# Centring two layer-norm tiles on VectorE and six on GpSimd, and one ScalarE table set for logarithm and exponential

## The chip, the cores and the metric

The kernel runs on one core of a Trainium2 chip. The metric is the device time of one execution in microseconds; the time of a kernel is the median of its runs.

The core has five engines that take their instructions in order and wait for each other by semaphores: TensorE (PE in the profile; PEld is its weight load), VectorE (DVE), ScalarE (ACT), GpSimd (POOL) and SyncE (SP, which only issues transfers).

## The reference

Two blocks are computed on one sequence of 512 tokens with 1024 features, in fp32. The first block has two layers of: RMS norm with modulation, an input projection, three mixers side by side (sliding-window attention, retention, gated linear attention), an output projection, an RMS norm and the residual. The second block has two layers, a mixer and a convolutional feed-forward each, and behind each of these four a layer norm:

```python
for l in range(DEPTH):
    y = even_mixer(x, ...) if l % 2 == 0 else odd_mixer(x, ...)
    x = layer_norm(alpha * x + y, ln_g[l, 0], ln_b[l, 0])
    y = conv_ffn(x, ffn_w_up[l], ffn_conv_w[l], ffn_conv_b[l], ffn_w_down[l])
    x = layer_norm(alpha * x + y, ln_g[l, 1], ln_b[l, 1])
return x
```

A layer norm subtracts the mean over the 1024 features from each token, divides by the root of the variance plus 1e-5, and applies a gain and a bias. An inverse root is computed as exp(-0.5 * ln(variance + eps)), so each norm takes one logarithm and one exponential.

## The kernel before

Activations lie transposed: `X` is 8 tiles (k = 0 to 7) of 128 features by 512 tokens. Every matrix product is made of three TensorE passes per weight tile (lines 902 to 904): an operand is split into a high part (`HI`, `WHI`, written by ScalarE) and the rest (`LO`, `WLO`, written by VectorE as a difference of two SBUF tiles). So each product needs ScalarE, then VectorE, then TensorE.

The program is a list of stages, and each engine runs through it with its own instruction stream. The stages that matter here are the four "tails" `even_out`, `down` (layer 0), `odd_out` and `down` (layer 1), each followed by the "head" of the next stage: `up` (0), `odd_in`, `up` (1) and `store`.

At the end of a tail TensorE sums mean and mean of squares over the features (lines 932 to 941). VectorE forms the variance (`RS`, line 2582), copies the mean from PSUM to SBUF (`MEAN`, line 2583), and subtracts it from tiles 0 to 3 (`centred`, line 2045, `N_CENTRED` = 4). Meanwhile ScalarE takes the logarithm (line 1470) and the exponential (line 1472). Then VectorE waits for that result (`rstd_known`).

At the head of the next stage, `normalised` on VectorE goes through the tiles: for k of 4 and more first the centring of tile k (line 2045), then gain times inverse root (`scalar_tensor_tensor`, line 2062), then the low part of tile k-1 (line 2053). Between the last two ScalarE adds the bias and writes the high part (line 1478). In the first three heads TensorE works three output tiles at once, staggered by one input tile (`first_jobs_of`): input step 0 has 3 passes, step 1 has 6, steps 2 to 7 have 9 each. In `store` there are no low parts: the tiles are shifted by ScalarE, transposed by TensorE (line 1429), copied (line 1940) and sent out.

TensorE issues `IDLE` matmuls that nobody reads (line 1443, two passes each) between a tail and the next head, so that it isn't idle there.

The other norms: the stage `out` ends in an RMS norm, `prenorm` (between the two layers of the first block) in another, both by `rstd` (lines 1470, 1472). The stage `mix` (twice) interleaves attention (exponentials, line 1704) with gated linear attention (line 1740 exponential, line 1742 logarithm) and two head norms (lines 1811, 1816 and 1861, 1863). `even_mix` has a head norm too (lines 1666, 1668). A function of ScalarE needs a table set; the build puts an `ACT_TABLE_LOAD` ahead of any function that the loaded set lacks, and `preload_act_table` puts one at a chosen place.

GpSimd issues 22 small loads in the first stages and has nothing after them.

Of the kernel before, what the change touches and what calls it, by code (L numbers as in the profile page):

```python
# [21 lines left out]
ACT = mybir.ActivationFunctionType  # L22
ALU = mybir.AluOpType
# [7 lines left out]
KD = D // P  # L31
# [12 lines left out]
WIDEST = 1280  # L44

NTILES = 34


def t5_bucket(dist):
# [91 lines left out]
def build(nc, io, cst, out, stop=None):  # L141

    ctx = ExitStack()
    with ctx:
# [11 lines left out]
        X = sb("X", [KD, T])  # L156
# [91 lines left out]
        MEAN = STAT[:, 3, :]  # L248
        SQM2 = STAT[:, 2:5:2, :]
        MEAN_PS, MSQ_PS = PS[:, 4, :], PS[:, 5, :]  # L250
# [45 lines left out]
        def sem(name):  # L296
            return ctx.enter_context(nc.semaphore(name))
# [23 lines left out]
            sem(f"at_{n}") for n in ("scores", "scaled", "exp", "probs", "turned", "turn_free", "values", "mixed"))  # L321

        sq_ready, sq_used, rstd_ready, normed = sem("sq_ready"), sem("sq_used"), sem("rstd_ready"), sem("normed")

        sub_sums, sub_rstd, sub_spread = sem("sub_sums"), sem("sub_rstd"), sem("sub_spread")

# [395 lines left out]

        BANKS = {"mod": len(VECTORS) + KD + len(HOT_CUTS), "mix": 4}

        IDLE = {"mod": 5, "prenorm": 6, "out": 7, "even_out": 7, "down": 7, "odd_out": 7, "odd_in": 3}

        HEADS_OF = {("up", 0): 0, ("odd_in", 0): 1, ("up", 1): 2, ("store", 0): 3}
        TAILS = ("out", "even_out", "down", "odd_out")
        HOLDS = ("proj", "even_in", "odd_up")
        N_CENTRED, LAG = 4, 3  # L730
        THREE = [("even_in", 0), ("up", 0), ("odd_in", 0), ("up", 1)]
        BEFORE_THREE = [stages[n - 1] for n in range(1, len(stages)) if stages[n] in THREE]

# [59 lines left out]
        @block.gpsimd  # L793
        def _(pool):
            n_const = [0]

            def load(dst, src):
                n_const[0] += 1
                pool.dma_start(dst, src).then_inc(const_in, 16)

            pool.dma_start(HOT, cst["onehot"]).then_inc(hot_in, 16)
            pool.dma_start(TABLE[0:32, :], io["rel_bias_2"]).then_inc(hot_in, 16)
            pool.wait_ge(pe_met, 1)
            pool.wait_ge(dve_met, 1)
            with nc.allow_non_contiguous_dma(reason="small operands, a feature to a partition"):
                for l in range(LAYERS):
                    load(SINKS[:, 8 * l:8 * l + 8], io["attn_sinks"][l].partition_broadcast(P))
                    for a in range(4):
                        load(GWB[l][32 * a:32 * a + 16, :], io["gla_gate_w"][l])
                    load(GWB[l][16:17, :], io["gla_gate_b"][l:l + 1])  # L810
                    for a in range(2):
                        load(GLAG[64 * a:64 * a + 64, l:l + 1], io["gla_norm_gain"][l].rearrange("(p o) -> p o", o=1))
                load(DECAY, cst["decay"])
                load(UPPER, cst["upper"])
                load(WINDOW, cst["window"])
                load(SUBM, cst["sub"])
                load(HEADS_32, cst["heads"])
                load(LAMP, io["ev_lambda_2"][0].rearrange("a b -> (a b)").partition_broadcast(P))
                N_CONST[0] = 16 * n_const[0]


        @block.sync
# [627 lines left out]
        def _(act):  # L1450
# [73 lines left out]
            def linear(jobs, l, tail=None, late=None, hold=False, early=False, three=False, to_three=False, loads=None):  # L1524
                n, upto = 0, at_split[0] + sum(len(j["chunks"]) for j in jobs if j["kind"] == "F") if hold else len(chunks)
                weights(at_split[0] + 1)
                for i, j in enumerate(jobs):
# [14 lines left out]
                    if j["by"] != "act":  # L1542
                        if j["how"] == "gate" if j["kind"] == "F" else False:
                            gelu(n - 1)
                        me.emptied_by(j["by"])
                        if tail is not None and j["kind"] == "F":
                            if j["n"] == KD - 1:
                                act.preload_act_table(ACT.Ln)
                                weights(at_split[0] + (3 if to_three else 2))
                            act.wait_ge(acc_free_dve, me.emptied["dve"])  # L1550
                            square(SQS[:, j["n"] % 2, :], j["dst"], j["n"], (sq_used, reused(tail, j["n"])))
                        continue
                    if tail is not None and j["n"] == KD - 1:
                        act.preload_act_table(ACT.Ln)
                    bank = take()
                    c = at_split[0]
                    if early and j["kind"] == "F" and c + 1 < len(chunks) and chunks[c + 1][2] - chunks[c - 1][2] <= SLOTS:
# [177 lines left out]
            def state_lane(l):  # L1735
# [89 lines left out]
                inputs(inputs_of("out")[0:3], True)  # L1825
                act.wait_ge(gla_near, NB * (l + 1))
                weights(at_split[0] + 2)
                act.preload_act_table(ACT.Ln)
                gla_mix(NB - 1)
                gla_squares(l)  # L1830
                inputs(inputs_of("out")[3:6], True, 3)
# [34 lines left out]
            for n_met, (s, l) in enumerate(stages, 1):  # L1866
# [6 lines left out]
                if s == "mod":  # L1873
                    for c0, n, src in VECTORS[0]:
                        act.dma_start(VROWS[c0:c0 + n, 0:P], src).then_inc(first_in, 16)
                    act.dma_start(IDN, cst["mats"][:, 0, :]).then_inc(first_in, 16)
                    act.dma_start(z(22).bitcast(I32), io["positions"][0].partition_broadcast(P)).then_inc(pos_in, 16)
                    act.dma_start(TINY[:, 4:7], cst["freq"]).then_inc(pos_in, 16)
                    w_mod = io["w_mod"][0]
                    act.dma_start(MATS[:, 1:8, :], cst["mats"][:, 1:8, :]).then_inc(mats_in, 16)  # L1880
                    for k in (1, 3, 5, 7):
                        act.dma_start(MOD_W[k], w_mod[k * P:k * P + P, 0:2048]).then_inc(mod_loaded[k], 16)
                    act.preload_act_table(ACT.Silu)
                    bank = take()
                    fn(VEC[:, 0:56], bank[:, 0:56], ACT.Copy).then_inc(me.signals(acc_free_act), 1)
                    act.wait_ge(*me.last)
                    fn(CACT, CT, ACT.Silu).then_inc(c_ready, 1)

                    def hot(k):
                        c, w = HOT_CUTS[k]  # L1890
                        bank = take()
                        fn(VECS_SB[:, c:c + w], bank[0:16, 0:w], ACT.Copy, scale=8.0).then_inc(me.signals(acc_free_act), 1)
                    for k in range(HOT_FIRST):
                        hot(k)
                    for k in range(KD):
                        me.emptied_by("dve")
                        act.wait_ge(acc_free_dve, me.emptied["dve"])
                        square(SQM2[:, k % 2, :], X[:, k, :], k, (sq_used, reused(0, k)))
                        if HOT_FIRST + k < len(HOT_CUTS):
                            hot(HOT_FIRST + k)  # L1900
                        if k == 3:
                            act.wait_ge(side_dve, me.after(side_dve, 2))
                        if k in (3, 4):
                            fn(ROPE[:, k - 3, :], z(27 - k), ACT.Sin).then_inc(me.signals(act_step), 1)
                    for group in VECTORS[1:]:
                        c0, n = group[0][0], sum(n for _, n, _ in group)
                        bank = take()
                        fn(VEC[:, c0:c0 + n], bank[:, 0:n], ACT.Copy).then_inc(me.signals(acc_free_act), 1)
                    act.wait_ge(*me.last)
                    act.dma_start(SCR, VECS_SB).then_inc(table_out, 16)  # L1910
                    act.wait_ge(msq_ready, me.after(msq_ready))
                    rstd(RS, MSQ_PS, EPS6)
                    act.wait_ge(mod_used, KD + 3)
                    for j in range(2):
                        r = slice(32 * j, 32 * j + 1)
                        fn(MOD_ROWS[r, :], PS[r, 4, :], ACT.Copy).then_inc(me.signals(mod_rows), 1)
                    weights(2)
# [6 lines left out]
                    act.wait_ge(msq_ready, me.after(msq_ready))  # L1924
                    rstd(RS, MSQ_PS, EPS6)
                elif s == "mix":
                    act.preload_act_table(ACT.Exp)
                    mixers(l)
                elif s in ("even_mix", "odd_mix"):
                    if s == "odd_mix":  # L1930
                        act.preload_act_table(ACT.Exp)
                    attention(UNITS[s])
                elif s == "even_sub":
                    head_squares([H[:, t, :] for t in range(4)], EPS5)
# [36 lines left out]
        def _(dve):  # L1971
# [70 lines left out]
            def centred(k):  # L2042

                dve.wait_ge(*me.last)
                tt(X[:, k, :], X[:, k, :], MEAN, ALU.subtract).then_inc(me.signals(dve_step), 1)  # L2045
# [9 lines left out]
            def normalised(n):  # L2055

                for k in range(KD + 1):
                    if k < KD:
                        if k >= N_CENTRED:
                            centred(k)  # L2060
                        dve.wait_ge(*me.last)
                        stt(X[:, k, :], X[:, k, :], LNG[:, n, k:k + 1], RS, ALU.mult, ALU.mult) \
                            .then_inc(me.signals(normed), 1)
                    if k == 2 and n < 3:
                        weights(at_split[0] + 3)
                    if k and n < 3:
                        low(k - 1, X[:, k - 1, :], LNB[:, n, k - 1:k])
# [389 lines left out]
            for n_met, (s, l) in enumerate(stages, 1):  # L2457
# [71 lines left out]
                else:  # L2529
# [46 lines left out]
                    elif s in TAILS:  # L2576
# [3 lines left out]
                        dve.wait_ge(mean_sq, me.after(mean_sq))  # L2580
                        dve.wait_ge(*me.last)
                        tt(RS, MSQ_PS, MEAN2, ALU.subtract).then_inc(me.signals(var_ready), 1)
                        nc.vector.tensor_copy(MEAN, MEAN_PS).then_inc(me.signals(dve_step), 1)
                        if (s, l) not in BEFORE_THREE:
                            weights(at_split[0] + 2)
                        for k in range(N_CENTRED):
# [48 lines left out]
```

## Time and profile before

| | |
|---|---|
| median of 3 runs | 2103.79 us (2102.29 to 2104.71) |
| the profiled execution | 2098.76 us, its span 2096.8 us |
| TensorE busy | 1991.4 us, 95% of the span |
| VectorE busy | 1089.2 us, 52% |
| ScalarE busy | 959.2 us, 46% |
| GpSimd busy | 12.7 us, 1% |
| granted TensorE clock, mean | 0.981 |

The span is the time between the first and the last instruction of the profiled execution; 2.0 us of its time lie outside. It is 5.0 us shorter than the median of the timed runs.

### The profile page before, as it was taken

The page shows a single profiled execution, that of the slowest core. Times are in us where ns is not written, and L with a number is a line of the kernel's source. Part 1 is how long each engine was busy: PE and PEld are TensorE (multiplying, and loading weights), DVE is VectorE, ACT ScalarE, POOL GpSimd, SP SyncE. Part 2 cuts the span into 40 slices and gives each one's busy share as a digit, 9 for nine tenths or more (in the row PEclk, how much of TensorE's full clock was granted, in tenths as well). Part 3 has the DMA queues.
Part 4 walks back from the last instruction along what each step waited for, and adds up shares of the span by engine and source line. Part 5 has one row for each costly group of instructions (what it writes and reads, how often), then busy time and mean ns, then how long its engine had stood idle before and what let it go on. Part 6 is the DMA issues. An engine that isn't in the chain of part 4 may idle for free.

```text
span 2096.8 us, 25344 instructions
## 1 busy us (share of the span) xinstructions
PE 1991.4 (95%) x9889; PEld 1484.4 (71%) x9889; DVE 1089.2 (52%) x2023; ACT 959.2 (46%) x1758; POOL 12.7 (1%) x28
## 2 busy tenths in 40 slices
PE   8999889999889999899999999999999999999997
PEld 4876446677456788566788888777666668888885
DVE  5623864632873422656665543452386575555343
ACT  4734764743674233574433222254587543232223
POOL 1000000000000000000000000000000000000000
PEclk8999999999989999999999999999999999999999
DMA  8431432223202433003233333325400123333331
GB/s 281 124 92 51 161 101 80 61 72 91 81 21 81 144 95 88 16 1 116 70 92 100 92 95 101 107 62 124 146 2 2 51 71 101 92 100 96 96 93 48
DMA packets 301267, 183.13 MB, mean 87 GB/s; under 512 B 17550, under 2 KB 292108, under 8 KB 299948
## 3 DMA queue, kind: packets, MB, share of 16 engines
q1 hardware_dynamic: 295437, 166.05, 27.2%
q10 hardware_dynamic: 4704, 13.31, 1.7%
q0 software_dynamic: 1008, 2.15, 0.3%
q8 instruction: 79, 1.29, 0.3%
q14 instruction: 39, 0.32, 0.0%
HBM read 179.22 MB, written 2.27 MB: 87 GB/s over the span
## 4 chain that ended last, share of the span: by engine, by line
PE 84%; DVE 8%; ACT 5%; issue 1%; DMA 1%; ACTq 0%; DVEq 0%
PE PS L902 22%; PE PS L904 22%; PE PS L903 22%; PE PS L1048 3%; PE PS L1076 2%; PE PS L1061 2%; DVE SE L2152 1%; PE PS L1202 1%; DVE WLO L2078 1%; PE PS L1014 1%; DVE X L2045 1%; PE PS L1120 1%; ACT WHI L1514 1%; PE PS L1225 1%; PE PS L1234 1%
## 5 line engine op out<-in xcount | busy, mean ns | idle before, releaser
L903 PE MATMUL PS<-LO,WHI 128*128 128x512 f32 x1690 | 659.7, 390 | 0.0
L902 PE MATMUL PS<-HI,WHI 128*128 128x512 f32 x1578 | 626.3, 397 | 24.9 <-DVE LO L2051 10.2
L904 PE MATMUL PS<-HI,WLO 128*128 128x512 f32 x1578 | 616.0, 390 | 0.0
L2078 DVE TENSOR_TENSOR WLO<-RING,WHI 128x1024 fp32r<-128x1024 f32 (+3 forms) x271 | 314.5, 1161 | 528.8 <-ACT WHI L1514 527.8
L1514 ACT ACTIVATE WHI<-RING 128x1024 fp32r<-128x1024 f32 (+3 forms) x271 | 272.7, 1007 | 468.2 <-PE PS L904 446.1
L902 PEld LDWEIGHTS PS<-HI,WHI 128*128 128x128 f32 x1578 | 297.2, 188 | 108.3 <-issue 26.8
L903 PEld LDWEIGHTS PS<-LO,WHI 128*128 128x128 f32 x1690 | 318.5, 188 | 65.0 <-issue 1.7
L904 PEld LDWEIGHTS PS<-HI,WLO 128*128 128x128 f32 x1578 | 297.1, 188 | 62.7
L902 PE MATMUL PS<-HIDDEN,WHI 128*128 128x512 f32 x352 | 137.1, 389 | 0.6 <-PE PS L904 0.6
L903 PE MATMUL PS<-HIDDEN,WHI 128*128 128x512 f32 x352 | 137.0, 389 | 0.0
L904 PE MATMUL PS<-HIDDEN,WLO 128*128 128x512 f32 x352 | 136.9, 389 | 0.0
L1621 ACT ACTIVATE S<-PS 128x512 f32<-128x512 f32 x44 | 26.3, 599 | 179.0 <-PE PS L904 179.0
L1641 ACT ACTIVATE SE<-SE,TINY 128x31 f32<-128x31 f32 (+7 forms) x176 | 96.6, 550 | 2.4 <-DVE TINY L2152 2.2
L1048 PE MATMUL PS<-Z 64*128 64x256 f32 (+7 forms) x416 | 84.3, 475 | 6.1 <-DVE TINY L2152 3.4
L1466 ACT ACTIVATE S<-X 128x512 f32<-128x512 f32 x48 | 30.3, 632 | 127.9 <-DVE X L2127 112.3
L2107 DVE TENSOR_SCALAR E<-S,VEC 128x512 f32<-128x512 f32 x44 | 24.1, 547 | 123.0 <-ACT S L1621 122.8
L902 PEld LDWEIGHTS PS<-HIDDEN,WHI 128*128 128x128 f32 x352 | 66.1, 188 | 15.1 <-issue 1.4
L1061 PE MATMUL PS<-MATS,SE 128*128 128x128 f32 (+1 forms) x420 | 67.9, 285 | 9.0 <-ACT ETW L1650 3.8
L904 PEld LDWEIGHTS PS<-HIDDEN,WLO 128*128 128x128 f32 x352 | 66.1, 188 | 13.9
L903 PEld LDWEIGHTS PS<-HIDDEN,WHI 128*128 128x128 f32 x352 | 66.1, 188 | 13.5
L1061 PEld LDWEIGHTS PS<-MATS,SE 128*128 128x128 f32 (+1 forms) x420 | 44.4, 141 | 41.7 <-issue 15.9
L2152 DVE CUSTOM_DVE_ANT_0 SE<-PS,BIAS 128x31 f32<-128x31 f32 (+4 forms) x144 | 50.9, 411 | 28.3 <-PE PS L1061 21.0
(341 smaller groups left out, 2325.2 us busy)
## 6 DMA issues: line engine op xcount, KB each, us to landing
RING<-in_ffn_w_up SPq DMA_DIRECT2D x88, 512.0 KB, 3.7
RING<-in_w_in SPq DMA_DIRECT2D x48, 512.0 KB, 3.8
RING<-in_w_mod SPq DMA_DIRECT2D x32, 512.0 KB, 4.3
RING<-in_ffn_w_down SPq DMA_DIRECT2D x32, 512.0 KB, 4.0
RING<-in_ev_w_in SPq DMA_DIRECT2D x30, 512.0 KB, 3.8
RING<-in_w_out SPq DMA_DIRECT2D x16, 512.0 KB, 4.5
RING<-in_od_w_in SPq DMA_DIRECT2D x15, 512.0 KB, 3.8
RING<-in_ffn_w_down SPq DMA_DIRECT2D x16, 384.0 KB, 3.4
```

Source lines behind the costliest of these rows:

```text
L902: mm(bank, WHI[i2][:, i, :], hi, start=(k == 0), stop=False)
L903: mm(bank, WHI[i2][:, i, :], lo, start=False, stop=False)
L904: return mm(bank, WLO[i2][:, i, :], hi, start=False, stop=last)
L1048: ins = mm(out, g["q"][a][k], g["k"][a][k], start=(k == 0), stop=(k == last))
L1061: ins = nc.tensor.transpose(PS[0:w, TURN_BANK[at], x * B:x * B + B], buf[:, c:c + w], IDN)
L1076: ins = mm(out, v, probs, start=(i < 2), stop=(i >= last))
L1466: fn(dst, src, ACT.Square).then_inc(me.signals(sq_ready), 1)
L1514: fn(WHI[pair][:, 0:raw.shape[1], :], raw, ACT.Copy).then_inc(w_hi, 1)
L1621: fn(GPAD[:, n % 2, 2:T + 2], bank, ACT.Copy).then_inc(me.signals(acc_free_act), 1)
L1641: fn(x, x, ACT.Exp, bias=UNIT_MAX[u["n"] % 3][:, at:at + 1], scale=-1.0, accum_out=UNIT_DEN[u["n"] % 3][:, at:at + 1]).then_inc(at_exp, 1)
L2078: tt(WLO[i2][:, 0:nk, :], raw, WHI[i2][:, 0:nk, :], ALU.subtract).then_inc(me.signals(w_split), 1)
L2152: nc.vector.tensor_tensor_reduce(buf[:, a, g["c"]:g["c"] + g["n"]], score, g["bias"][:, a, :], -u["scale"], first, ALU.add, ALU.min, nmax[ ...
```

## The change

- `N_CENTRED` goes from 4 to 2: VectorE centres tiles 0 and 1. GpSimd, at each of the four layer norms, waits for the copy of the mean (`mean_copied`) and centres tiles 2 to 7, signalling `tile_centred` after each. VectorE waits for that signal ahead of line 2062 where it centred before.
- Before every logarithm and exponential the set `natural_log_exp_and_others`, which has both, is loaded, in place of the set of one function. One such load is new: in the stage `mod`, ahead of the wait for its sum.
- The unread matmuls become fewer: 6 to 4 after `prenorm`, 7 to 6 after `out`, 7 to 5 after the four tails.

```diff
+LN_EXP = "natural_log_exp_and_others"
...
+        mean_copied, tile_centred = sem("mean_copied"), sem("tile_centred")
...
-        IDLE = {"mod": 5, "prenorm": 6, "out": 7, "even_out": 7, "down": 7, "odd_out": 7, "odd_in": 3}
+        IDLE = {"mod": 5, "prenorm": 4, "out": 6, "even_out": 5, "down": 5, "odd_out": 5, "odd_in": 3}
...
-        N_CENTRED, LAG = 4, 3
+        N_CENTRED, LAG = 2, 3
...
+            centrings = [s for s, _ in stages if s in TAILS and s != "out"]
+            for n in range(len(centrings)):
+                pool.wait_ge(mean_copied, n + 1)
+                for k in range(N_CENTRED, KD):
+                    nc.gpsimd.tensor_tensor(X[:, k, :], X[:, k, :], MEAN, op=ALU.subtract).then_inc(tile_centred, 1)
...
-                                act.preload_act_table(ACT.Ln)
+                                act.preload_act_table_set(LN_EXP)
                                 weights(at_split[0] + (3 if to_three else 2))
...
-                        act.preload_act_table(ACT.Ln)
+                        act.preload_act_table_set(LN_EXP)
...
                 weights(at_split[0] + 2)
-                act.preload_act_table(ACT.Ln)
+                act.preload_act_table_set(LN_EXP)
                 gla_mix(NB - 1)
...
                     act.dma_start(SCR, VECS_SB).then_inc(table_out, 16)
+                    act.preload_act_table_set(LN_EXP)
                     act.wait_ge(msq_ready, me.after(msq_ready))
...
                 elif s == "mix":
-                    act.preload_act_table(ACT.Exp)
+                    act.preload_act_table_set(LN_EXP)
...
                     if s == "odd_mix":
-                        act.preload_act_table(ACT.Exp)
+                        act.preload_act_table_set(LN_EXP)
...
                         if k >= N_CENTRED:
-                            centred(k)
+                            dve.wait_ge(tile_centred, me.after(tile_centred))
                         dve.wait_ge(*me.last)
...
-                        nc.vector.tensor_copy(MEAN, MEAN_PS).then_inc(me.signals(dve_step), 1)
+                        nc.vector.tensor_copy(MEAN, MEAN_PS).then_inc(me.signals(mean_copied), 1)
```

## Rows read from the trace of the kernel before

**Rows 1.** The page: busy time and instructions of each engine.
```profile
PE 1991.4 (95%) x9889; PEld 1484.4 (71%) x9889; DVE 1089.2 (52%) x2023; ACT 959.2 (46%) x1758; POOL 12.7 (1%) x28
```

**Rows 2.** Timeline at the first layer norm: start us, us, what [idle before <-releaser].
```profile
989.43 6.25 PE L1443 MATMUL PS<-MATS 128*128 128x512 f32 x14
989.93 0.68 DVE L2583 COPY S<-PS 128x512 f32<-128x512 f32 x1
...
990.65 2.87 DVE L2045 TENSOR_TENSOR X<-X,S 128x512 f32<-128x512 f32 x4
990.79 1.28 ACT L1472 ACT_TABLE_LOAD   x1
...
992.08 0.63 ACT L1472 ACTIVATE RS<-RS 128x512 f32<-128x512 f32 x1
...
993.87 1.54 DVE L2062 SCALAR_TENSOR_TENSOR X<-X,VEC,RS 128x512 f32<-128x512 f32 x2
...
994.74 1.43 ACT L1478 ACTIVATE HI<-X,VEC 128x512 fp32r<-128x512 f32 x2 [2.03 <-DVE X L2062]
995.50 0.75 DVE L2053 SCALAR_TENSOR_TENSOR LO<-X,VEC,HI 128x512 fp32r<-128x512 f32 x1
...
996.50 0.47 PE L902 MATMUL PS<-HI,WHI 128*128 128x512 f32 x1 [0.82 <-DVE LO L2053]
```

**Rows 3.** Chain that ended last, input steps 1 to 6: start us, us, what.
```profile
997.75 0.50 PE PS L902
...
998.71 0.23 PE PS L902
...
999.41 0.29 PE PS L902
...
1008.04 0.35 PE PS L902
```

**Rows 4.** Timeline at the last layer norm, same columns as rows 2.
```profile
2074.79 2.87 DVE L2045 TENSOR_TENSOR X<-X,S 128x512 f32<-128x512 f32 x4
...
2077.90 3.12 DVE L2062 SCALAR_TENSOR_TENSOR X<-X,VEC,RS 128x512 f32<-128x512 f32 x4 [0.24 <-DVE X L2045]
...
2086.31 0.75 DVE L2062 SCALAR_TENSOR_TENSOR X<-X,VEC,RS 128x512 f32<-128x512 f32 x1
```

**Rows 5.** Timeline of VectorE: one subtraction over four times the data.
```profile
277.92 2.29 DVE L2321 TENSOR_TENSOR GPROD<-GPROD,Z 128x2048 f32<-128x2048 f32 x1
```

**Rows 6.** Chain that ended last: table load at the end of `out`, layer 0.
```profile
354.29 1.28 ACT L1472
```

**Rows 7.** Timeline at the end of prenorm.
```profile
369.44 1.28 ACT L1470 ACT_TABLE_LOAD   x1
369.48 1.13 PE L946 MATMUL PS<-S,MATS 128*128 128x512 f32 x2 [0.39 <-ACT S L1466]
370.74 0.69 ACT L1470 ACTIVATE RS<-PS,TINY 128x512 f32<-128x512 f32 x1
```

**Rows 8.** Timeline: TensorE's first matmuls behind the loads of the mixers.
```profile
198.26 0.66 PE L1129 MATMUL PS<-MATS,E 128*128 128x128 f32 x4 [0.41 <-ACT E L1722]
...
284.71 1.13 PE L1225 MATMUL PS<-GQ_OWN,BIAS 128*128 128x512 f32 x2 [0.97 <-ACT Z L1767]
...
615.71 0.66 PE L1141 MATMUL PS<-ET,Z 128*64 128x128 f32 x8 [0.98 <-ACT H L1716]
...
631.67 0.50 PE L902 MATMUL PS<-HI,WHI 128*128 128x512 f32 x1 [0.24 <-DVE LO L2051]
...
936.90 3.34 PE L1076 MATMUL PS<-ETW,Z 128*64 128x128 f32 x40 [2.20 <-ACT H L1657]
```

**Rows 9.** Timeline after the head of even_in: two passes at the lower clock.
```profile
686.89 0.63 PE L903 MATMUL PS<-LO,WHI 128*128 128x512 f32 x1
...
687.32 0.63 PE L904 MATMUL PS<-HI,WLO 128*128 128x512 f32 x1
```

## The prediction

> **What bounds the kernel now.** I read the page first: TensorE is busy for 95% of the span, GpSimd for 1% [rows 1]. That share contains the unread matmuls, so I went on to the chain of work that ended last. Nearly all of it is TensorE's; it leaves TensorE only where a stage's operand isn't there yet. The change touches such places alone, so I read the timeline at each. What a stage is worth is then how much earlier TensorE's next needed matmul can start.
>
> At the first layer norm [rows 2] the mean is in SBUF at 990.62. VectorE then centres four tiles until 993.52, while ScalarE has taken its logarithm, a table load of 1.28 and the exponential by 992.71. So VectorE is last there, by 0.8, and ScalarE's load is covered by it. Behind the stage's meeting point comes line 2062 at 993.87 (0.35 later), ScalarE's high part, the low part, and TensorE at 996.50. The unread matmuls end at 995.68 and hold nobody up. In the head VectorE takes 2.17 per tile (0.76 + 0.72 + 0.69), TensorE's nine passes take nine times 0.227, or 2.04; the first pass of each of steps 2 to 6 therefore stands in the chain with 0.29 to 0.36 where an ordinary one has 0.23 (first and last of the five in [rows 3]). The other two heads repeat this.
>
> At the last norm everything is VectorE's: from 2074.79 four centrings, four scalings, then four pairs, to 2087.06; ScalarE's last shift and all that sends the rows out hang on it [rows 4].
>
> **Part 1, centring in the first three heads.** VectorE does two centrings instead of four ahead of line 2062: 2 x 0.725 = 1.45 less. That uncovers ScalarE unless its load goes too: with it the inverse root is there at 992.71 and only 0.8 is gained; without it at 991.42, ahead of VectorE's new end at 992.07. So the gain is 1.45, and the load removed at these norms is worth 0.65 of it, not 1.28. In steps 2 to 6 VectorE's time falls from 2.17 to 1.5 per tile, under TensorE's 2.04, and these five excesses (0.06 to 0.13, 0.10 on average) go: 0.5. Together 1.95 per head, 5.85 for three.
>
> **Part 2, the last norm.** VectorE's chain from 2074.79 becomes 2 x 0.725 + 0.23 + 8 x 0.785 = 7.95 instead of 12.3: 4.35 less, if GpSimd keeps up. ScalarE's shift takes 0.72, under the pace of 0.785 [rows 2, 4].
>
> **Part 3, GpSimd's six subtractions.** The trace has none. Nothing else is in GpSimd's queue by then; its loads end in the first 60 us. Lower bound: VectorE's row for the same operation, 0.69 [rows 2]. Upper bound: four times as slow, VectorE's 2.29 for four times the data [rows 5]. Call it P. VectorE needs tile 2 at 994.8, so P can be 4 there, and TensorE needs tile 7 only by 1007.9. At 2.29 tile 7 is ready at 1004.4: the three heads lose nothing at either end. The last norm needs tile 7 at 2081.95, so from P = 1.18 on each 0.1 costs 0.6; at 2.29 it gains nothing and ends 2.3 later than before. I take P = 1.2, between the ends and nearer to the row of the same size, since the engine does ordinary elementwise work too: gain 4.2. The Trainium skill, GPSIMD Engine Reference, section "Elementwise — side-by-side cycle accounting", gives 4.5 us for a two-input operation on 2048 elements; a quarter of that is 1.12, an estimate by which the sum would be 0.15 better. No row here shows it.
>
> **Part 4, the table loads.** Those that end a wait of TensorE, with what TensorE can gain:
> - `out` of both layers: the load lies in the chain between logarithm and exponential, at 354.29 [rows 6] and again at 674.69: 1.28 each, 2.56.
> - `prenorm`: the load ahead of the logarithm starts at 369.44, but the last sum of squares ends at 370.60 and the logarithm starts at 370.74 [rows 7]: hidden, 0. The second one, between logarithm and exponential, is bare: 1.28.
> - `mix`, layer 0: the load at line 1742 delays a matmul that was held 0.41; its return load at line 1704 is covered by a wait for VectorE. The one at line 1811 delays one held 0.97 [rows 8], the one at 1816 none. Sum 1.38. Layer 1: 0.41 again, 0.98 at line 1816, 0.24 at line 1863 [rows 8]. Sum 1.63.
> - `even_mix`: TensorE stood 2.20 behind both loads [rows 8]; the first is hidden behind the sum of squares, the second is bare: 1.28.
> - `mod` and the preloads behind a product: they lie ahead of waits for TensorE, 0 either way. Should a preload of a set that is already there vanish, at most 0.4 more.
>
> Sum 8.1. Bounds: 5.1 if the mixers give nothing back, since their lanes are interleaved and another may be next; the full 1.28 for the ten loads in the mixers would make it 17.9, but TensorE's idle time ahead of the held matmuls doesn't allow that. The nearest rows allow 8.1.
>
> In the trace the load is 1.28 and the next instruction starts at once [rows 2]. The Trainium skill, ScalarE: Activation LUTs, section "What ACT_TABLE_LOAD costs", adds a drain of about 1.38 to each switch; by that rule the six bare loads of this part would return 8 us more. The trace shows no gap for it on either side of the load, so the sum goes by the trace.
>
> **Part 5, fewer unread matmuls.** Each has two passes of 0.43. In the heads they now end at about 993.95, and TensorE's first needed one starts at 995.05: a gap of 1.1 where 0.82 stood. They are in nobody's way before, so leaving them out gains 0. What they cover is the clock: in `even_in`, after gaps of 0.9 and 2.1, passes come at 0.43 instead of 0.23 [rows 9], which is the 1.2 GHz level in place of 2.4. I take 0, as gap and shift are nearly equal.
>
> **Sum.** 5.85 + 4.2 + 8.1 = 18.1. Against the profiled execution, 2098.76 (span 2096.8), that gives 2080.6; the median before lies 5.0 above it, and 2103.79 - 18.1 = 2085.7 is the forecast.
>
> **The rivals.**
>
> *The two engines shut each other out (slower).* Every VectorE instruction in a head reads two SBUF tiles, and so does GpSimd's. If only one of the two can run at a time and they alternate, VectorE's seven instructions up to the second low part (5.3 with gaps) have all six of GpSimd's between them. At P = 1.2 the first low part ends 8.6 after the mean and TensorE starts 2.8 late; step 1 starts at 1003.2 instead of 997.75; VectorE is then ahead again and step 7 starts 4.8 late. Three times 4.8 and 2.6 at the last norm make 17.0, less 8.1: +8.9, 2112.7. In general 17.0 + 24 x (P - 1.2): it decides from P = 0.83 on, and at 0.69 it would end at 2100.4. Against it, no row shows GpSimd reading while VectorE works; for it, none shows the opposite. The Trainium skill, SBUF — State Buffer, section "Who interferes with whom", states just this rule: an operation of VectorE with two SBUF inputs and one of GpSimd that reads SBUF block each other fully. It is the strongest thing against the change. Chance 0.25, of which 0.03 fall to a P small enough to be faster and 0.03 to no difference.
>
> *GpSimd only gets VectorE's gaps.* Then tiles 4 to 7 are waited for one by one, 2.7 per tile instead of 2.17: +2.6 per head, +2.3 at the end, together +10.1, less 8.1: 2105.8. Chance 0.05.
>
> *They share.* VectorE's seven instructions become a quarter longer while GpSimd works, 1.4, which eats the norms' gain; the tables stay: 2095.7. Chance 0.15.
>
> *The tables don't follow.* If the build still loads the logarithm's own set, no load goes and the heads gain 0.8 + 0.5, the last norm 3.5: -7.4, 2096.4. Chance 0.04.
>
> *The clock falls in the heads.* If at the six shortened places some 3 us run at the lower level, 1.5 is lost at each: -18.1 + 9 = -9.1, 2094.7. Chance 0.08.
>
> The forecast keeps 0.43.
>
> **How the numbers follow.** The forecast's own range is 2081 to 2090: the mixers at nothing (+3.0), the last norm with a slower P (+1.5), some 4 us the other way for clock and mixers. The whole range goes up to 2108, over sharing, clock, gaps and part of the shut-out case; what it leaves out is the shut-out case at P of 1.2 and more, about 0.19. A measurement of this kernel can tell about 0.2%, 4.2 us. Faster: 0.43 + 0.15 + 0.04 + 0.08 + 0.03 = 0.73. Same: 0.05 + 0.03 = 0.08. Slower 0.19.
>
> **What would show it.** Right: line 1472 has no table load; line 2062 starts 1.8 after the mean's copy; VectorE's instructions in the heads keep 0.69 to 0.75; GpSimd's six follow each other at P, under 1.2; TensorE's first matmul in `up` comes 1.45 earlier after the copy; the last norm's chain is 8 long. Wrong: VectorE's 0.75 become 1.5 to 2 right where a subtraction of GpSimd runs, or line 2062 waits for `tile_centred`; or passes of 0.43 spacing at the heads; or gaps in the mixers that stay as they were, with another releaser.

## The result: slower by 0.3%, and the profile after

The changed kernel took 2108.85 us in the median of 11 runs (2105.09 to 2113.13), the kernel before 2101.51 beside it (11 runs, 2096.27 to 2108.04). The ratio is 1.0028 with a 95% interval of 1.0016 to 1.0041: slower by 3 to 9 us. The forecast was 2085.7, and the range it came with went up to 2108. The profiled execution took 2106.57, its span is 2104.6 (2096.8 before), and the mean granted clock is 0.975 (0.981 before).

The page of the changed kernel, busy time and instructions of each engine; it answers to [rows 1]:

```profile
PE 1984.6 (94%) x9865; PEld 1486.9 (71%) x9865; DVE 1092.8 (52%) x1999; ACT 932.8 (44%) x1737; POOL 53.3 (3%) x52
```

VectorE has 24 instructions fewer and is busy for 3.6 us longer. GpSimd's 24 new ones cost it 40.6, as the changed kernel's groups by line tell (count, then busy and mean ns of one, then the idle time before them):

```profile
L827 POOL TENSOR_TENSOR X<-X,S 128x512 f32<-128x512 f32 x24 | 40.6, 1722 | 1994.5 <-DVE S L2592 1994.5
```

Where that comes from is seen at the first layer norm, in the timeline of the changed kernel; it answers to [rows 2]:

```profile
980.33 4.53 PE L1451 MATMUL PS<-MATS 128*128 128x512 f32 x10
980.82 0.68 DVE L2592 COPY S<-PS 128x512 f32<-128x512 f32 x1
980.94 0.72 ACT L1478 ACTIVATE RS<-RS,TINY 128x512 f32<-128x512 f32 x1 [0.99 <-DVE RS L2591]
981.54 2.37 DVE L2054 TENSOR_TENSOR X<-X,S 128x512 f32<-128x512 f32 x2
981.59 10.13 POOL L827 TENSOR_TENSOR X<-X,S 128x512 f32<-128x512 f32 x6 [925.34 <-DVE S L2592]
981.69 0.63 ACT L1480 ACTIVATE RS<-RS 128x512 f32<-128x512 f32 x1
...
984.26 2.98 DVE L2071 SCALAR_TENSOR_TENSOR X<-X,VEC,RS 128x512 f32<-128x512 f32 x2
987.17 1.75 DVE L2062 SCALAR_TENSOR_TENSOR LO<-X,VEC,HI 128x512 fp32r<-128x512 f32 x1
989.02 1.58 DVE L2071 SCALAR_TENSOR_TENSOR X<-X,VEC,RS 128x512 f32<-128x512 f32 x1
989.17 0.77 PE L910 MATMUL PS<-HI,WHI 128*128 128x512 f32 x1 [4.32 <-DVE LO L2062]
...
990.52 1.75 DVE L2062 SCALAR_TENSOR_TENSOR LO<-X,VEC,HI 128x512 fp32r<-128x512 f32 x1
992.33 0.80 PE L910 MATMUL PS<-HI,WHI 128*128 128x512 f32 x1 [1.54 <-DVE LO L2062]
992.38 0.75 DVE L2071 SCALAR_TENSOR_TENSOR X<-X,VEC,RS 128x512 f32<-128x512 f32 x1
```

ScalarE's load between logarithm and exponential is gone (the one starts at 980.94, the other at 981.69), and VectorE does two centrings, as forecast. But GpSimd's six subtractions take 10.13, and while they run VectorE's instructions take 1.31 to 1.75 each instead of 0.69 and 0.75; only the very first, which starts 0.05 ahead of GpSimd's first, takes 0.69. The next one, at 992.38, when GpSimd's last is nearly over, takes 0.75 again. No wait for GpSimd's signal `tile_centred` is shown there. The needed matmuls (lines 910 to 912; 902 to 904 before) start 8.96 after the variance's start (980.21), where it was 7.18 before.

The chain that ended last, in the changed kernel, from input step 1 on (start us, us, what), which answers to [rows 3]:

```profile
992.33 0.80 PE PS L910
993.12 0.43 PE PS L911
...
994.83 0.43 PE PS L912
995.26 0.34 PE PS L910
...
995.83 0.23 PE PS L912
```

Step 1 comes 12.1 after the variance instead of 8.4, and its passes have a spacing of 0.43. The granted clock is 0.50 of the full one from 989 to 995, which is the 1.2 GHz level instead of 2.4, in a head that had no such pass before. I count 6, 9 and 12 of them in the three heads.

From one variance to the next, and from the last to the end, the profiles give (us):

| from, to | before | changed | difference |
|---|---|---|---|
| start to first variance | 989.32 | 980.21 | -9.1 |
| first to second | 372.78 | 377.27 | +4.5 |
| second to third | 338.57 | 343.83 | +5.3 |
| third to fourth | 372.79 | 378.47 | +5.7 |
| fourth to the end | 23.33 | 24.85 | +1.5 |

Ahead of the norms some 9 us are gained, and at the norms 17.0 are lost. The first row is not to be trusted by itself: in the profiles of the kernels below that have the same tables the first variance starts anywhere from 979.99 to 986.73. The other four repeat: 377.28, 344.01, 378.41 and 24.82 in the same kernel with longer rows of unread matmuls.

### The profile page after: what moved, and what is told of

Its sections match the earlier page's. It is cut to its first block, busy times and chain, and to the rows that moved or that the text cites. A ratio compares the mean times of both kernels' runs of the same rounds, so it can differ in the third digit from the quotient of the medians.

```text
span 2104.6 us, 25301 instructions
## 1 busy us (share of the span) xinstructions
PE 1984.6 (94%) x9865; PEld 1486.9 (71%) x9865; DVE 1092.8 (52%) x1999; ACT 932.8 (44%) x1737; POOL 53.3 (3%) x52
## 3 DMA queue, kind: packets, MB, share of 16 engines
q8 instruction: 79, 1.29, 0.3%
## 4 chain that ended last, share of the span: by engine, by line
PE 84%; DVE 9%; ACT 4%; issue 1%; DMA 1%; ACTq 0%; DVEq 0%
PE PS L910 22%; PE PS L912 22%; PE PS L911 22%; PE PS L1056 3%; PE PS L1084 2%; PE PS L1069 2%; DVE X L2071 1%; DVE SE L2161 1%; PE PS L1210 1%; DVE WLO L2087 1%; DVE LO L2062 1%; ACT WHI L1522 1%; PE PS L1233 1%; PE PS L1242 1%; PE PS L1022 1%
## 5 line engine op out<-in xcount | busy, mean ns | idle before, releaser
L910 PE MATMUL PS<-HI,WHI 128*128 128x512 f32 x1578 | 627.3, 398 | 40.6 <-DVE LO L2062 22.6
L827 POOL TENSOR_TENSOR X<-X,S 128x512 f32<-128x512 f32 x24 | 40.6, 1722 | 1994.5 <-DVE S L2592 1994.5
```

The source lines that it names most:

```text
L827: nc.gpsimd.tensor_tensor(X[:, k, :], X[:, k, :], MEAN, op=ALU.subtract).then_inc(tile_centred, 1)
L910: mm(bank, WHI[i2][:, i, :], hi, start=(k == 0), stop=False)
```

## The experiments

**Each half alone.** The tables alone: six centrings back to VectorE, the rows of unread matmuls as before.

```diff
-        N_CENTRED, LAG = 2, 3
+        N_CENTRED, LAG = 4, 3
...
-                    nc.gpsimd.tensor_tensor(X[:, k, :], X[:, k, :], MEAN, op=ALU.subtract).then_inc(tile_centred, 1)
...
-                            dve.wait_ge(tile_centred, me.after(tile_centred))
+                            centred(k)
```

> Only the table set changes; VectorE centres all eight tiles, GpSimd does nothing, the unread matmuls are as before. Both theories (engines shut each other out; slow GpSimd) price the tables alike: about 8 to 9 us faster than before (the traces of before and after differ by 9.1 at the table load ahead of the first layer norm), ratio 0.996, and nothing gained at the four layer norms, since VectorE's four centrings are last there. If the ratio is 1.000, the tables gain nothing and the loss at the norms is smaller than I read.

Measured: 2091.73, ratio 0.9955 (0.9938 to 0.9972), so -9.5 us (5.9 to 13.0). The tables are worth what Part 4 said.

The centring alone: the functions' own sets again, and the rows of unread matmuls as before.

```diff
-                                act.preload_act_table_set(LN_EXP)
+                                act.preload_act_table(ACT.Ln)
...
-        IDLE = {"mod": 5, "prenorm": 4, "out": 6, "even_out": 5, "down": 5, "odd_out": 5, "odd_in": 3}
+        IDLE = {"mod": 5, "prenorm": 6, "out": 7, "even_out": 7, "down": 7, "odd_out": 7, "odd_in": 3}
```

> Only the centring moves to GpSimd; tables and unread matmuls as before. Shut-out theory: each head about 4 to 5 us later, the last norm 1 to 2, together some 15 to 17 us slower, ratio about 1.007 to 1.008; the table load between logarithm and exponential stays hidden, because VectorE's second centring now ends 2.4 after the first begins. Rival, that the loss is all the clock (the shorter row of unread matmuls): then this run, which has the long row, loses only 10 or less.

Measured: 2117.31, ratio 1.0078 (1.0061 to 1.0094): +16.4. With the tables' -9.5 that makes +6.9, or 1.0033, where the whole change has 1.0028. The parts add up, within their intervals, and the loss is all in the centring. (Both halves have the long rows, so the closest whole is the next kernel, with 1.0038.) This kernel too has passes at the lower clock in its heads (10, 12 and 13), and it has the long rows of unread matmuls.

**The length of the rows.** The change with the rows of before.

```diff
-        IDLE = {"mod": 5, "prenorm": 4, "out": 6, "even_out": 5, "down": 5, "odd_out": 5, "odd_in": 3}
+        IDLE = {"mod": 5, "prenorm": 6, "out": 7, "even_out": 7, "down": 7, "odd_out": 7, "odd_in": 3}
```

> The changed kernel with the long rows of unread matmuls of before. Theory of two causes: the heads' passes come at 0.23 spacing again instead of 0.43, 1 to 2 us back in each of three heads, 3 to 6 us in all, ratio about 1.000 to 1.001 against before. Rival, that TensorE's 4 us of waiting in the head drops the clock whatever stands in front: then nothing comes back, ratio 1.003 as for the change.

Measured: 2111.33, ratio 1.0038 (1.0024 to 1.0053). Nothing comes back. Its timeline at the first norm:

```profile
980.34 6.25 PE L1451 MATMUL PS<-MATS 128*128 128x512 f32 x14
...
989.19 0.76 PE L910 MATMUL PS<-HI,WHI 128*128 128x512 f32 x1 [2.60 <-DVE LO L2062]
989.75 0.63 PE L911 MATMUL PS<-LO,WHI 128*128 128x512 f32 x1
```

TensorE still stands for 2.60, and the first passes are slow whatever ran before: 7, 10 and 11 in the three heads. So the lower clock isn't due to the shorter rows.

**The two engines one after the other.** VectorE waits for all six of GpSimd's subtractions before its own two.

```diff
-                        if k >= N_CENTRED:
-                            dve.wait_ge(tile_centred, me.after(tile_centred))
...
                         nc.vector.tensor_copy(MEAN, MEAN_PS).then_inc(me.signals(mean_copied), 1)
+                        dve.wait_ge(tile_centred, me.after(tile_centred, KD - N_CENTRED))
```

> The changed kernel, but VectorE waits for all six of GpSimd's subtractions before its own first one, so GpSimd runs alone. Shut-out theory: the six take about 0.95 each (the alternating pair takes 1.68, less VectorE's 0.73), 5.7 in all, and VectorE's instructions are back at 0.69 to 0.75; the head costs about as much as with both at once. Rival, that GpSimd simply needs 1.7 for such a tile and only VectorE is held up: then the six take 10.2 here too.

Measured: one time, 2119.16. Its timeline at the first norm:

```profile
984.61 7.37 POOL L827 TENSOR_TENSOR X<-X,S 128x512 f32<-128x512 f32 x6 [926.45 <-DVE S L2590]
...
992.02 1.42 DVE L2054 TENSOR_TENSOR X<-X,S 128x512 f32<-128x512 f32 x2 [7.49 <-POOL X L827]
993.79 1.54 DVE L2069 SCALAR_TENSOR_TENSOR X<-X,VEC,RS 128x512 f32<-128x512 f32 x2
```

Alone, GpSimd takes 7.37 for six, one every 1.225, and VectorE has its 0.69 and 0.75 back. So each lengthens the other, and neither is slow by itself. The expected 0.95 each (5.7 for six) was missed: it took an alternating pair, 1.68, for the sum of two times that don't overlap at all. The head takes longer than with both at once: the first needed matmul starts 13.2 after the variance, against 8.96. In the change a pair of instructions, one of each engine, takes 1.675 (from line 2062 at 987.17 to line 2062 at 990.52 are two pairs). In turns that never touched it would be 1.225 + 0.73 = 1.95, so about 0.28 of GpSimd's 1.225 lies beside VectorE's work and 0.95 does not, an estimate.

**One operand of VectorE in PSUM.** If what collides is the reading of two SBUF operands, VectorE's instructions should be free once one of the two is in PSUM. VectorE now centres with the mean where TensorE left it, and ScalarE's exponential goes to a free bank of PSUM, from which line 2071 of the change (2072 here) reads it. The low parts (2062, here 2063) keep their two SBUF inputs.

```diff
+        RS_PS = PS[:, 6, :]
...
-                fn(dst, dst, ACT.Exp, scale=-0.5).then_inc(me.signals(rstd_ready), 1)
+                fn(dst if to is None else to, dst, ACT.Exp, scale=-0.5).then_inc(me.signals(rstd_ready), 1)
...
-                    rstd(RS, RS, EPS5)
+                    rstd(RS, RS, EPS5, RS_PS)
...
-                tt(X[:, k, :], X[:, k, :], MEAN, ALU.subtract).then_inc(me.signals(dve_step), 1)
+                tt(X[:, k, :], X[:, k, :], MEAN_PS, ALU.subtract).then_inc(me.signals(dve_step), 1)
...
-                        stt(X[:, k, :], X[:, k, :], LNG[:, n, k:k + 1], RS, ALU.mult, ALU.mult) \
+                        stt(X[:, k, :], X[:, k, :], LNG[:, n, k:k + 1], RS_PS, ALU.mult, ALU.mult) \
```

> The changed kernel; VectorE's centring now reads the mean from PSUM and the scaling of line 2062 an inverse root that ScalarE writes to PSUM, so both have one SBUF operand and only the low parts have two. Theory that the shut-out comes from the second SBUF operand: VectorE's centrings and scalings go back to 0.69 and 0.75, only low parts beside GpSimd stay long (up to 1.7), the last norm is free of it (its chain after the variance is about 9.6 long instead of 15.2) and the whole is about 17 us faster than before, ratio 0.992. Rival, that VectorE is held up by any work of GpSimd: instructions stay at 1.6, ratio 1.003 as for the change.

Measured: 2085.86, ratio 0.9919 (0.99 to 0.9938): 17 us faster than before, 23 faster than the change. First the changed kernel, then this one, grouped by line while GpSimd works (busy, mean ns of one | idle before):

```profile
L2071 DVE SCALAR_TENSOR_TENSOR X<-X,VEC,RS 128x512 f32<-128x512 f32 x3 | 4.5, 1508 | 0.2
L2062 DVE SCALAR_TENSOR_TENSOR LO<-X,VEC,HI 128x512 fp32r<-128x512 f32 x2 | 3.5, 1749 | 0.0
L2054 DVE TENSOR_TENSOR X<-X,S 128x512 f32<-128x512 f32 x2 | 2.3, 1166 | 0.1
```

```profile
L2072 DVE SCALAR_TENSOR_TENSOR X<-X,VEC,PS 128x512 f32<-128x512 f32 x5 | 3.7, 747 | 0.4
L2063 DVE SCALAR_TENSOR_TENSOR LO<-X,VEC,HI 128x512 fp32r<-128x512 f32 x4 | 3.7, 933 | 0.1
L2055 DVE TENSOR_TENSOR X<-X,PS 128x512 f32<-128x512 f32 x2 | 1.4, 686 | 0.1
```

The instructions with one SBUF operand keep the time they had before (0.75 and 0.69) beside a working GpSimd, with 747 and 686 ns; the low parts take 933. They still collide, and here GpSimd pays most of it: in this head its first three subtractions take 1.27 each, and the last three, each of which meets a low part, 1.73 to 1.74. At the last norm, where there are no low parts, VectorE's eight scalings and GpSimd's six run side by side:

```profile
2068.10 7.43 POOL L828 TENSOR_TENSOR X<-X,S 128x512 f32<-128x512 f32 x6 [362.63 <-DVE S L2593]
...
2069.70 6.63 DVE L2072 SCALAR_TENSOR_TENSOR X<-X,VEC,PS 128x512 f32<-128x512 f32 x8 [0.24 <-DVE X L2055]
```

GpSimd's row is as long as when it is alone (7.43 against 7.37). The changed kernel has for the same two:

```profile
2081.14 10.15 POOL L827 TENSOR_TENSOR X<-X,S 128x512 f32<-128x512 f32 x6 [368.32 <-DVE S L2592]
...
2083.71 10.70 DVE L2071 SCALAR_TENSOR_TENSOR X<-X,VEC,RS 128x512 f32<-128x512 f32 x8 [0.24 <-DVE X L2054]
```

Here is the cause shown: the same instructions on the same engines, one operand of each moved, and the loss turns into the gain that was forecast.

**What GpSimd must do to collide.** VectorE centres all eight tiles itself. GpSimd works on 464 spare columns, with work that nobody uses: fills at the first norm, copies at the second, two-input subtractions at the third and fourth.

```diff
+                    if n == 0:
+                        nc.gpsimd.memset(SPARE, 0.0).then_inc(tile_centred, 1)
+                    elif n == 1:
+                        nc.gpsimd.tensor_copy(SPARE, flat[:, 0:464]).then_inc(tile_centred, 1)
+                    else:
+                        nc.gpsimd.tensor_tensor(SPARE, flat[:, 0:464], flat[:, 0:464], op=ALU.subtract).then_inc(tile_centred, 1)
```

> Tables as in the change, VectorE centres all eight tiles from SBUF, and GpSimd does six idle operations on 464 columns of a spare tile at each norm, one after the other: a fill (no input) at the first, a copy of a constant tile at the second, a difference of two inputs at the third and fourth. Theory that GpSimd's reads are what collides: VectorE stays at 0.69 to 0.75 at the first norm and is held up at the third and fourth; the second tells whether one input suffices (I expect it does). Rival, that any instruction of GpSimd holds VectorE up: all four norms show 1.4 to 1.7.

Measured: one time, 2101.86. Groups by line at the first, second and third norm, each from a window of its own:

```profile
L831 POOL MEMSET SPARE<- 128x464 f32 x6 | 2.9, 485 | 926.3 <-DVE S L2600 926.0
L2062 DVE TENSOR_TENSOR X<-X,S 128x512 f32<-128x512 f32 x4 | 2.8, 692 | 0.1
...
L833 POOL COPY SPARE<-MATS 128x464 f32<-128x464 f32 x6 | 5.7, 956 | 369.9 <-DVE S L2600 369.6
L2062 DVE TENSOR_TENSOR X<-X,S 128x512 f32<-128x512 f32 x4 | 3.5, 878 | 0.1
...
L835 POOL TENSOR_TENSOR SPARE<-MATS 128x464 f32<-128x464 f32 x6 | 7.9, 1315 | 334.4 <-DVE S L2600 334.0
L2062 DVE TENSOR_TENSOR X<-X,S 128x512 f32<-128x512 f32 x4 | 4.7, 1171 | 0.1
```

VectorE's subtraction takes 0.692 beside fills, 0.878 beside copies and 1.171 beside subtractions (mean of four). In the timeline the ones that have GpSimd at work for their whole length take 0.69, 0.94 and 1.33. So GpSimd's writing costs VectorE nothing, and each stream that it reads costs something. The two engines read different tiles here (`MATS` against `X` and `MEAN`), so it isn't that they share one. VectorE's first subtraction, which starts 0.02 to 0.05 ahead of GpSimd's instruction, keeps its 0.69 at every norm; at the third GpSimd's first takes 1.46 in its place, and its next ones 1.29.

**VectorE from PSUM without GpSimd.** Reading from PSUM might be the whole gain. VectorE centres all tiles with the mean from PSUM; the copy is gone, the tables stay.

```diff
-                tt(X[:, k, :], X[:, k, :], MEAN, ALU.subtract).then_inc(me.signals(dve_step), 1)
+                tt(X[:, k, :], X[:, k, :], MEAN_PS, ALU.subtract).then_inc(me.signals(dve_step), 1)
...
-                        nc.vector.tensor_copy(MEAN, MEAN_PS).then_inc(me.signals(mean_copied), 1)
```

> Tables as in the change, no work of GpSimd, unread matmuls as before; VectorE centres all eight tiles straight from the mean in PSUM, and the copy of the mean goes. The copy took 0.61 of the chain at each of four norms: 2.4 us on top of the 9.5 of the tables, ratio 0.994. It is what the idea has to be beaten by: if e7_act_copy isn't faster than this, GpSimd brings nothing even without the shut-out.

Measured: 2091.67, ratio 0.9947 (0.9928 to 0.9966), which can't be told from the tables alone (0.9955). From the last variance to the end it takes 23.19, against 23.80 for the tables alone and 19.84 with GpSimd; in the first head the first needed matmul starts 6.56 after the variance, against 7.18 and 5.91. So the missing copy gives 0.6 at each norm, and the operand in PSUM by itself nothing. All six times with GpSimd (2082.71 to 2088.52) lie below all six of this kernel (2088.72 to 2095.20), 5.8 apart in the medians. That much is GpSimd's.

**The copy to ScalarE.** ScalarE copies the mean for GpSimd while VectorE forms the variance, so VectorE's copy (0.68) is off its path.

```diff
                     fn(MEAN2, MEAN_PS, ACT.Square).then_inc(me.signals(mean_sq), 1)
+                    fn(MEAN, MEAN_PS, ACT.Copy).then_inc(me.signals(mean_copied), 1)
...
-                        nc.vector.tensor_copy(MEAN, MEAN_PS).then_inc(me.signals(mean_copied), 1)
+                        dve.wait_ge(mean_copied, me.after(mean_copied))
```

> As e5_psum, but ScalarE copies the mean to SBUF right after squaring it, while TensorE's last sum runs, so GpSimd starts some 1.6 earlier and VectorE has no copy. Shut-out by SBUF operands: first needed matmul about 5.7 after the variance starts (before 7.2, changed 9.0), last norm's chain 8.8 after the variance instead of 13.6 before; about 10 us at the norms and 9.5 from the tables, ratio 0.990 to 0.991. If low parts are held up more than once each, 0.993.

Measured: 2089.63, ratio 0.9931 (0.9908 to 0.9953); the gain hoped for isn't there. The last norm takes 18.80 after the variance, 1.0 less than 19.84, as expected. But the heads don't follow. Timeline at the first one:

```profile
986.75 1.63 DVE L2064 SCALAR_TENSOR_TENSOR LO<-X,VEC,HI 128x512 fp32r<-128x512 f32 x1
...
988.63 0.47 PE L911 MATMUL PS<-HI,WHI 128*128 128x512 f32 x1 [1.42 <-DVE LO L2064]
...
990.12 0.50 PE L911 MATMUL PS<-HI,WHI 128*128 128x512 f32 x1 [0.55 <-DVE LO L2064]
...
990.98 0.63 PE L911 MATMUL PS<-HI,WTHIRD 128*128 128x512 f32 x1
```

The first low part falls on a subtraction of GpSimd that started 0.18 before it, and takes 1.63, so the first needed matmul starts 6.07 after the variance and not 5.7. The last of these rows, with its 0.63, is where the clock falls to the 1.2 GHz level (granted 0.50), for six or seven passes in each head. TensorE had stood 1.42 behind the unread matmuls. Two kernels followed from this, and both have the long rows again. The first is otherwise the same:

> As e7_act_copy, with the long rows of unread matmuls of before. In e7_act_copy TensorE stood 1.42 behind the short row and some ten passes then came at 0.43 spacing; in e5_psum it stood 1.27 and they did not. Theory that the idle time behind the row decides: with the long row no pass is slow, the three heads take 1.3 less each, ratio 0.991. Rival, that the row is irrelevant, as it was for the changed kernel: ratio 0.993 again.

Measured: 2085.09, ratio 0.9912 (0.9899 to 0.9926), with no pass at the lower clock in any head, and the head's 72nd pass 23.5 after the variance where it was 24.7. Its timeline:

```profile
984.39 6.25 PE L1452 MATMUL PS<-MATS 128*128 128x512 f32 x14 [0.15 <-PE PS L950]
...
990.35 0.51 PE L911 MATMUL PS<-HI,WHI 128*128 128x512 f32 x1
990.93 0.40 PE L913 MATMUL PS<-HI,WLO 128*128 128x512 f32 x1
```

TensorE goes over from the unread matmuls to the needed ones with no idle time shown. The profile shows what was meant; the intervals of the two ratios overlap, so the timed runs alone don't prove that it pays.

The second has VectorE centre three tiles and GpSimd five:

```diff
-        N_CENTRED, LAG = 2, 3
+        N_CENTRED, LAG = 3, 3
```

> As e7_act_copy, with three tiles on VectorE and five on GpSimd and the long rows of unread matmuls. GpSimd is then done about when the first low part starts, so that one or two low parts collide instead of three, and the clock holds: first needed matmul 6.0 after the variance starts, the 72nd at 23.3; the last norm ends as in e7_act_copy. About 19 us faster than before, ratio 0.991. If the clock falls all the same, 0.993.

Measured: 2087.0, ratio 0.992 (0.9905 to 0.9935), with no slow pass; the last norm is 0.65 longer than with two (19.46 against 18.81), near VectorE's one more subtraction. The three best kernels, 2085.86, 2085.09 and this one, can't be told apart by their intervals.

## Why the prediction was wrong, point by point

**The step that failed** is the assumption behind Parts 1 to 3 that the two engines work side by side at their own speeds. It held 0.43 against 0.25 for "The two engines shut each other out", on the ground that "no row shows GpSimd reading while VectorE works; for it, none shows the opposite". There was no row on either side, and the odds went to the side without a rule. The centring alone costs 16.4 (2117.31), with one operand in PSUM it gains, and it costs nothing beside fills: that is the shut-out, by what each engine reads from SBUF. The Trainium skill, SBUF — State Buffer, section "Who interferes with whom", says that a VectorE instruction with two SBUF inputs contends with a GpSimd instruction that reads SBUF, and doesn't with one that only writes; and that VectorE with at most one SBUF input doesn't contend. The traces agree with all three (1.31 to 1.75 for 0.69 and 0.75; 0.692; 0.747 and 0.686). "Fully", in the prediction's words for it, goes too far here: a pair takes 1.675, not 1.95. The section calls the contention an exclusive lock, but has the words "fully blocks" for another case, VectorE's 2-port modes.

**Part 1 and Part 2.** The gains of 1.95 per head and 4.2 at the last norm were sized well for a kernel in which the engines don't meet. With the operand in PSUM the first needed matmul starts 5.91 after the variance (7.18 before: -1.3, forecast -1.45), step 1 7.41 (8.43 before: -1.0, since a low part of 0.93 lies between), the 72nd pass, the last of the first three output tiles (3 x 8 x 3), 23.34 (24.63 before: -1.3, forecast -1.95), and the last norm takes 19.84 (23.33 before: -3.5, forecast -4.2). Three times 1.3 and 3.5 make 7.4; the timed runs have 7.6 between the tables alone and this kernel (0.9955 and 0.9919). Of the forecast 10.05 three quarters are there to be had.

**Part 3.** P is 1.225, taken 1.2. It was right, and it was the wrong thing to size with care. The estimate by the Trainium skill, GPSIMD Engine Reference, section "Elementwise — side-by-side cycle accounting", 1.12, is 0.1 too low.

**Part 4.** 8.1 against 9.5 measured, with 5.9 to 13.0: right as a sum. The places are right in part. From `out` of layer 0 to the first layer norm the forecast's terms make 6.75. Measured between the same two passes (at 330.16 and 985.20 in the trace before), that stretch took 655.6 before, and 647.3 to 648.0 in all ten kernels with the new tables: 7.5 to 8.3 less. `even_mix` gives 1.28 as said: TensorE's wait there falls from 2.20 [rows 8] to 0.92. Around it the stretches at the lower clock moved, which I had not seen. The 40 small matmuls behind the wait took 3.34 and now take 2.40, but that is no gain: two groups ahead of the wait now take 1.89 and 2.35 where they took 1.14 and 1.53, since the 3.4 us of granted clock 0.50 lie before the wait (from 923.7) instead of behind it (from 938.2). What the clock gives is a second such stretch, from 948.4 before, that is gone: 1.0.

```profile
611.39 0.66 PE L1149 MATMUL PS<-ET,Z 128*64 128x128 f32 x8 [0.98 <-ACT H L1724]
...
930.44 2.40 PE L1084 MATMUL PS<-ETW,Z 128*64 128x128 f32 x40 [0.92 <-ACT H L1665]
```

These are rows of the changed kernel. The first shows the opposite: in `mix`, layer 1, the wait that should have given 0.98 is 0.98 still. Up to there and to the end of the mixers the changed kernel gained 0.2; the wait of 0.24 at 631.67 is gone, which makes it 0.8 in all where 1.63 was forecast. What the wait of 0.98 hangs on instead is not shown. For layer 0 I can't say: from the pass at 189.95 of the trace before, where its mixers begin, to the one at 300.85 it took 110.9 before and 107.6 to 116.0 in the ten kernels with the new tables. A preload of the set that is already there didn't vanish: 22 loads of 1.28 are left of 43. No drain as the Trainium skill, ScalarE: Activation LUTs, section "What ACT_TABLE_LOAD costs", has it, shows up in the timed gain: with the prediction's 8 us on top the tables would have been worth 16, above the interval's 13.0. Part 4 itself has four loads at the full 1.28, though, and not six; for those alone the drain would be 5.5, an estimate, and the sum 13.6, just above the interval. The trace is the stronger witness: in `even_mix` one bare load less gave 1.28 and no more.

**Part 5.** "I take 0" for the clock was wrong, but not for the reason weighed there. The heads run 6, 9 and 12 passes at 0.43 instead of 0.23, or 27 x 0.20 = 5.4 us. The heads bear this out: the third has six slow passes more than the first, and its 72nd pass starts 30.27 after the variance instead of 29.08, or 0.20 for each. The shorter rows aren't the cause, since with the long ones nothing comes back (2111.33). What comes with the slow passes is TensorE standing 2.6 to 4.3 ahead of the head and again 1.5 to 2.2 between its first steps, which is a consequence of the shut-out. The second stand isn't needed for it: where TensorE stood 8.5 (the engines one after the other) or 4.1 (GpSimd's idle subtractions, third head) and then had no such gap, 8 to 11 passes were slow.

**The rival's size.** It had 17.0 at P = 1.2 and the norms lost 17.0, but this is luck in part. With 0.95 as the exclusive time in place of 1.2, its formula gives 17.0 + 24 x (0.95 - 1.2) = 11.0. The clock's 5.4, which it didn't have, make 16.4. Its first step, TensorE 2.8 late, is really 1.8; step 1, forecast 5.45 late, is 3.7.

**What stays open.** After 1.42 of idle time behind the unread matmuls six or seven passes ran at the lower clock, after 1.27 in a kernel with nearly the same head none did, and after 1.84 (GpSimd's idle copies, second head) none did either. So the length of the stand alone doesn't decide it, and I can't derive which of the two a kernel will get. It is also not shown why 0.28 of GpSimd's instruction lies free.

## What to carry to other kernels

Before VectorE's elementwise work is shared out to GpSimd, count the SBUF operands of every VectorE instruction that will run meanwhile: with two of them, and a GpSimd that reads, both engines slowed down here, and an engine at 1% in the page is no free engine. Move one of VectorE's operands to PSUM where it comes from TensorE or ScalarE anyway; here that turned +0.3% into -0.8%, of which the tables alone are -0.45%. And where neither side of an assumption has a row, a rule of the Trainium skill that says just this about these operands deserves more than even odds, and the sum should then include what a late TensorE does to its clock.

## What the runs showed of the hardware

- Two-SBUF-input instructions of VectorE (128x512, fp32) alternate with GpSimd's subtractions at 1.675 us a pair, against 0.69 to 0.75 and 1.225 alone.
- Against 464 columns of GpSimd's work, VectorE's subtraction of two SBUF tiles takes 0.69 beside fills, 0.94 beside copies, 1.33 beside two-input subtractions.
- With one operand in PSUM it takes 0.686 beside a working GpSimd (0.686 to 0.689 without one), the scaling 0.747. A low part with two SBUF inputs between such instructions takes 0.93 instead of 0.75, while the subtraction of GpSimd that meets it takes 1.73 instead of 1.27; where GpSimd's had started 0.18 before, the low part took 1.63.
- TensorE's granted clock fell to 0.50 (1.2 GHz) in every head of a layer norm where it had stood for 2.6 to 8.5 us, and in one kernel after 1.42; it stayed up after 0.82, 1.27 and 1.84, and where the unread matmuls reached to the first needed one.
- A table load took 1.28 also where the set was already there (22 loads in the changed kernel), and the next instruction followed at once.
